# Four modulation chunks moved between the feature products, folded in a kept PSUM bank

## The reference

```python
mod = (silu(c) @ w_ada + b_ada).reshape(b, 6, D_MODEL)      # w_ada (1024, 6144)
sh1, sc1, g1, sh2, sc2, g2 = [mod[:, j] for j in range(6)]
proj = (x * (1.0 + sc1) + sh1) @ w_in                       # -> z, xbc, dt, rg_x, rg_gate, q, k, v, g
...                                                         # the three mixers
x  = layernorm(ALPHA * x + (1.0 + g1) * (mixers @ w_out))
h2 = x * (1.0 + sc2) + sh2                                  # router, top-2 experts
x  = layernorm(ALPHA * x + (1.0 + g2) * moe(h2))
```

## Time and profile before

| | us |
|---|---|
| median of 3 runs | 2025.87 (2024.02 to 2026.23) |
| the profiled execution | 2027.97 |
| its span in the trace | 2026.2 |
| PE busy | 1626.1 (80%) |
| DVE busy | 761.2 (38%) |
| ACT busy | 347.1 (17%) |
| DMA, mean over the span | 280 GB/s |

### The profile page before, as it was taken

One profiled execution on the slowest core, in us unless ns is written; L12 is line 12 of the kernel. 1 busy time (PEld: TensorE's weight loads), 2 busy tenths in 40 slices (PEclk: granted clock), 3 DMA queues, 4 the chain that ended last, 5 costly groups with the idle time before them and its releaser, 6 DMA issues.

```text
span 2026.2 us, 29151 instructions
## 1 busy us (share of the span) xinstructions
PE 1626.1 (80%) x11574; PEld 881.1 (43%) x11574; DVE 761.2 (38%) x1701; ACT 347.1 (17%) x791; POOL 113.7 (6%) x162
## 2 busy tenths in 40 slices
PE   4999999898866767767699999989886766777782
PEld 1775534443533333334277553344353433333341
DVE  0254636437522212222436364453762211222235
ACT  0235211102111110110123521110211110111000
POOL 3001012010100000000020000201000000000000
PEclk8899988859888878888979989895989888888896
DMA  9332344573699999999943243548259999999992
GB/s 331 115 126 75 99 140 135 180 278 149 253 427 427 429 428 428 429 429 428 391 153 125 88 125 86 174 163 299 101 243 427 427 429 428 428 428 429 429 427 96
DMA packets 93461, 567.51 MB, mean 280 GB/s; under 512 B 7061, under 2 KB 7917, under 8 KB 68034
## 3 DMA queue, kind: packets, MB, share of 16 engines
q1 hardware_dynamic: 81666, 532.06, 64.6%
q0 software_dynamic: 11712, 34.32, 6.1%
HBM read 550.54 MB, written 15.81 MB: 280 GB/s over the span
## 4 chain that ended last, share of the span: by engine, by line
PE 46%; DMA 37%; DVE 9%; issue 2%; ACT 2%; DVEq 2%; SPq 2%; POOL 0%; ACTq 0%; POOLq 0%
DMA ring<-in_exp_w_up 35%; PE ps L1367 10%; PE ps L894 8%; PE ps L918 8%; PE ps L1106 3%; PE ps L901 2%; PE ps L791 2%; PE ps L1056 1%; PE ps L1225 1%; PE ps L1181 1%; PE ps L1076 1%; PE ps L1342 1%; PE ps L1281 1%; DMA r0s<-in_state_ret 1%; DMA ring<-in_w_ada 1%
## 5 line engine op out<-in xcount | busy, mean ns | idle before, releaser
L1367 PE MATMUL ps<-ring,xTb 128*32 128x256 f32 x4224 | 328.6, 479 | 238.9 <-DMA ring<-in_exp_w_up 233.5
L1367 PEld LDWEIGHTS ps<-ring,xTb 128*32 128x32 f32 x4224 | 163.6, 137 | 403.3 <-issue 359.3
L2414 DVE TENSOR_TENSOR hb<-sg,ps 128x128 f32<-128x128 f32 x66 | 25.0, 379 | 493.0 <-ACT sg L1704 493.0
L918 PE MATMUL ps<-ring,hT 128*128 128x512 f32 x384 | 178.0, 621 | 0.0
L894 PE MATMUL ps<-hT,ring 128*128 128x288 f32 x640 | 163.6, 415 | 4.6 <-ACT hT L1487 3.5
L1342 PE MATMUL ps<-sel,h_tm 128*128 128x128 f32 (+1 forms) x912 | 163.2, 306 | 0.0
L1342 PEld LDWEIGHTS ps<-sel,h_tm 128*128 128x128 f32 x912 | 125.1, 189 | 53.8 <-issue 27.2
L894 PEld LDWEIGHTS ps<-hT,ring 128*128 128x128 f32 x640 | 122.7, 195 | 39.5 <-issue 6.5
L1381 PE MATMUL ps<-ring,hTb 128*32 128x256 f32 x2112 | 129.9, 387 | 6.0 <-DVEq L2417 3.8
L918 PEld LDWEIGHTS ps<-ring,hT 128*128 128x128 f32 x384 | 75.2, 200 | 107.4 <-issue 106.1
L1704 ACT ACTIVATE sg<-ps 128x128 f32<-128x128 f32 x66 | 18.3, 277 | 596.2 <-PE ps L1367 596.2
(11 more groups left out here) (412 smaller groups left out, 1750.5 us busy)
## 6 DMA issues: line engine op xcount, KB each, us to landing
ring<-in_exp_w_gate SPq DMA_DIRECT2D x66, 2048.0 KB, 18.8
ring<-in_exp_w_up SPq DMA_DIRECT2D x66, 2048.0 KB, 23.2
ring<-in_exp_w_down SPq DMA_DIRECT2D x66, 2048.0 KB, 24.7
ring<-in_w_ada SPq DMA_DIRECT2D x24, 2048.0 KB, 11.0
ring<-in_w_in SPq DMA_DIRECT2D x22, 2048.0 KB, 8.3
ring<-in_w_out SPq DMA_DIRECT2D x8, 2048.0 KB, 10.0
h0s<-in_state_ssd POOLq DMA_DIRECT2D x16, 512.0 KB, 6.9
out_ssd_s<-h0s POOLq DMA_DIRECT2D x16, 512.0 KB, 5.3
```

Of the source, the lines that this page charges most:

```text
L918: last = mm(o[:, :], hT[:, k, T0[i]:T0[i] + P], w[:, k, :], start=(k == 0), stop=(k == KT - 1))
L1367: last = mm(ps[32 * j:32 * j + 32, b, 0:2 * P], xTb[:, k, m * BLK:(m + 1) * BLK], w[:, 0:2, k * D_EXPERT + j * P:k * D_EXPERT + (j + 1) * ...
```

## The change

Chunks 4 to 7 leave the retention. Chunk 4, 5 and 6 are multiplied behind the feature products m = 3, 7 and 11 (and the transposes that follow these), chunk 7 behind the dt product and the state transposes, ahead of the gate products. Their ScalarE copies go to two places in turn (`spare`), so two by two they are folded at once: `fold_ada(4)` ahead of chunk 6 and `fold_ada(6)` behind the gate products add up the four strips with the constant `fold` and leave each chunk's 9 rows in a quarter (32 partitions) of PSUM bank 7. Bank 7 keeps all four until ScalarE copies it once, in the retention's second step, to `adaf`. `spread` then reads chunks 4 to 7 from 32 rows of `adaf`. Chunks 8 and 9 take the places of 4 and 5 at the end of `ret(1)`, 10 and 11 stand in the session loop behind b = 2 and b = 4. The ring's order and the bank plan follow.

```diff
-STREAM: ... + [("in", C_XBC + CH * n) for n in range(3)] + [("in", C_Z), ("in", C_Z + CH)] ... [("ada", n) for n in range(4, 12)] ...
+STREAM: ... + [x for n in range(3) for x in (("in", C_XBC + CH * n), ("ada", 4 + n))] + [("ada", 7)]
+          + [("in", C_Z), ("in", C_Z + CH)] ... [("ada", n) for n in range(8, 12)] ...
+        adaf = qkvg[:, 0, 0:CH]
@@ tensor: spread
-                        pe.wait_ge(*takes(l, ("ada", c)))
+                        if c < 8:
+                            pe.wait_ge(adaf_ready.sem, adaf_ready.at(l, 1))
+                        else:
+                            pe.wait_ge(*takes(l, ("ada", c)))
...
+                        lo, hi = (32 * (c - 4), 32 * (c - 3)) if c < 8 else (0, P)
+                        src = adaf[lo:hi, :] if c < 8 else ada_at(c)
+                        mm(o[:, :], C("fold", P, 0, 1)[lo:hi, :].to_broadcast([hi - lo, P]), src, start=True, stop=True
+                           ).then_inc(FL, 1)
+                def fold_ada(c):
+                    for j in (c, c + 1):
+                        pe.wait_ge(*takes(l, ("ada", j)))
+                    idle["pe"].stand(pe)
+                    for j in (c, c + 1):
+                        last = mm(ps[32 * (j - 4):32 * (j - 3), 7, :], C("fold"), ada_at(j), start=True, stop=True,
+                                  skip_group_check=True)
+                    return last
@@ tensor: features, behind the transposes of m
+                    if m in (3, 7, 11):
+                        if m == 11:
+                            fold_ada(4)
+                        ada(4 + m // 4, n)
+                        free_slot(n)
+                        n += 1
@@ tensor: behind the state transposes / behind the gate products
+                ada(7, n)
+                free_slot(n)
+                n += 1
+                fold_ada(6).then_inc(ada_folded.sem, 1)
@@ tensor: session loop; end of ret(1)
-                            if 1 <= b <= 6:
-                                ada_here(5 + b)
+                            if b in (2, 4):
+                                ada_here(9 + b // 2)
-                        ada_here(4)
-                        ada_here(5)
+                        ada_here(8)
+                        ada_here(9)
@@ scalar: in the feature loop; behind the tail copies; retention
+                    if m in (3, 7, 11):
+                        take_ada((4 + m // 4,))
+                take_ada((7,))
-                        take_ada(range(6, 12))
+                        take_ada((10, 11))
-                        take_ada((4, 5))
+                        act.wait_ge(ada_folded.sem, ada_folded.at(l, 1))
+                        cp(adaf, ps[:, 7, :]).then_inc(adaf_ready.sem, 1)
+                        take_ada((8, 9))
```

More of the change, by code:

```diff
@@ L73 @@
 STREAM = ([("ada", n) for n in range(4)] + [("in", C_RGX), ("in", C_RGG)]
-          + [("in", C_XBC + CH * n) for n in range(3)] + [("in", C_Z), ("in", C_Z + CH)]
-          + [("in", C_Q + CH * n) for n in range(4)] + [("out", 0), ("out", 1)]
-          + [("ada", n) for n in range(4, 12)] + [("out", 2), ("out", 3)])
+          + [x for n in range(3) for x in (("in", C_XBC + CH * n), ("ada", 4 + n))] + [("ada", 7)]
+          + [("in", C_Z), ("in", C_Z + CH)] + [("in", C_Q + CH * n) for n in range(4)] + [("out", 0), ("out", 1)]
+          + [("ada", n) for n in range(8, 12)] + [("out", 2), ("out", 3)])
 QUAD = 4
@@ L130, in ret_steps @@
             out.append((("rt", b), "D"))
-            if 1 <= b <= 6:
-                out.append((("ada", 5 + b), "A"))
+            if b in (2, 4):
+                out.append((("ada", 9 + b // 2), "A"))
     if i == 0:
@@ L138, in ret_steps @@
     if i == 1:
-        out += [(("ada", 4), "A"), (("ada", 5), "A")]
+        out += [(("ada", 8), "A"), (("ada", 9), "A")]
     return out
@@ L155, in bank_plan @@
             out.append((("xst", m - 3), "A"))
+        if m in (3, 7, 11):
+            out.append((("ada", 4 + m // 4), "A"))
     out += [(("tail", q), "A") for q in range((XT + RT) // 4)]
-    out += [(("dt",), "D"), (("h0rg",), "D")]
+    out += [(("dt",), "D"), (("h0rg",), "D"), (("ada", 7), "A")]
     out += [(("rga", m), "A") for m in range(RT)] + [(("rgi", m), "A") for m in range(RT)]
@@ L465, in trunk @@
         gate_used = sig("gate_used", 1)
+        ada_folded = sig("ada_folded", 1)
+        adaf_ready = sig("ada_folded_taken", 1)
         small_in = sig("small_in", 16 * 13)
@@ L807, in spread @@
                     for j, c in enumerate(cs):
-                        last = mm(o[32 * j:32 * j + TS, :], C("gs"), ada_at(c), start=True, stop=True, skip_group_check=True)
+                        lo, hi = (32 * (c - 4), 32 * (c - 3)) if c < 8 else (0, P)
+                        src = adaf[lo:hi, :] if c < 8 else ada_at(c)
+                        last = mm(o[32 * j:32 * j + TS, :], C("gs")[lo:hi, :], src, start=True, stop=True, skip_group_check=True)
                     last.then_inc(FL, 1)
+                def fold_ada(c):
[6 more added lines that the diff above has]
+                    return last
                 def free_slot(n):
@@ L1110, in ada_here @@
                 def ada_here(c):
-                    ada(c, n_ada + c - 4)
-                    free_slot(n_ada + c - 4)
+                    ada(c, n_ada + c - 8)
+                    free_slot(n_ada + c - 8)
                 for i in range(2):
@@ L1215, in _ @@
                 idle["pe"].stand(pe)
-                n = n_ada + 8
+                n = n_ada + 4
                 w = [stream(n), stream(n + 1)]
```

3 lines of the change are left out of this document (1 added, 2 removed).

## The result

The changed kernel took 2031.41 us, the median of 16 runs (2026.82 to 2040.08), against 2024.2 us for the kernel before in as many runs on the same chip (2018.11 to 2028.22): ratio 1.0036, 95% interval 1.0022 to 1.0050. It is slower, by a little more than the 0.2% that tell a change from none. It is 4.3 us above the forecast of 2027.1, and that understates the miss: the forecast had +1.2 us over the kernel before, and the medians of the sixteen runs stand 7.2 us apart. The profiled executions hide it: the one after took 2027.69 us (span 2025.7), the one before 2027.97 us (span 2026.2), one of the fastest of the one kernel and one of the slowest of the other.

A forecast was written before the change was run, and what follows sets the result against it. TensorE was taken to bound the mixer's feature products and half-clock session loop. Per layer 10.9 + 0.3 less 10.7 or 10.5 gave +1.2 us together, 2027.1 against the median 2025.87; range 2020 to 2035.

The forecast's parts named there:

- The likeliest case: Whole kernel: chunks cost in the features about what the session loop gives back, 2027.1 us; chance 0.48.
- Sessions without a chunk: Retention's session loop: a session that carries no chunk takes 4.33 us, DVE's chain setting the pace, clock at half.
- The wait for the states: Session loop: reloaded states come late at the last session, 0 to 0.5 us lost, 0.3 taken per layer.
- The features with the second fold: Feature stage up to z, both folds included: the moved chunks add 10.9 us per layer.
- Transposes to tails: Features' end, chunk 6 and first fold: 4.3 us after, 3.2 before, so 1.1 us is paid.
- Chunks 4 and 5: Behind feature products 3 and 7: each costs the full 2.57 us, 5.1 us for two.
- Chunk 7 at half clock, copy and table load exposed: Around the gate products: chunk 4.15 us at half clock, then 5.65 us of ACT's queue before the seventh gate product.
- z starts: Features' end: z's products begin 11.7 us after chunk 7 begins, second fold included, against 7.0 before.
- Rival (b): z products: clock falls after the stall before the seventh gate product; 3.3 us per layer, 2033.7, one layer 2030.4; chance 0.22.
- I take 0, nearest to the row: Spread of chunks 4 and 5 after the session loop: reading 32 rows instead of 128 changes nothing in sum.
- Both of its bounds: Spread of chunks 4 and 5: products side by side win 1.6 us; a clock returning later costs 1.7.
- The spread of 6 to 9 lies beside DVE's LayerNorm and counts for nothing: Later spread of modulation chunks 6 to 9: it runs beside DVE's work, so its change adds 0 us.

## Why the prediction came out as it did

The likeliest case (an even exchange, within 0.2%) did not come; the time is 0.36 and 0.30% above the kernel before, inside the range given and on its slower side. The stages give +5.0 us where the forecast had +1.2. By the steps:

- Sessions without a chunk, 4.33 us, DVE next: right, in all four layers. The wait for the states: right in kind, hidden in part behind what DVE had taken; the loop gave 0.4 us per layer more than forecast.
- The features with the second fold: +11.8 for +10.9. Transposes to tails: right (4.21 against 4.3). Chunks 4 and 5: the products behind chunk 5 lie 2.73 us later against those ahead of it, where 2.57 was forecast. Chunk 7 at half clock, copy and table load exposed: right in both layers (the seventh gate product 9.81 and 10.09 us after chunk 7's start, forecast 9.80), though its wait is 2.43 or 0.72 us depending on the gates' own clock. That z starts 11.6 and 11.2 us behind chunk 7 for 11.7 is a match by the mark alone, as the fold lies behind it and not ahead.
- Rival (b), the clock falling behind that wait: it came in layer 0, where the wait was the longer, and not in layer 1. The last gate products took 1.79 us there and 1.14 in layer 1, fold and z together 3.77 (172.03 to 175.80) and 2.77. The price was some 1.7 us, not 3.3, since the clock was 0.98 from 174 on. That the measured 2031.4 lies near this rival's 2030.4 for one layer is luck: most of the loss is elsewhere.
- The step that failed: "I take 0, nearest to the row", for the spread and what stands behind it. Both of its bounds came true at once: the products side by side (2.08 us for 3.31) and the later clock, under which the sample rows took 1.92 for 1.05 and the first output products 5.64 for 3.70. -1.23 + 0.87 + 1.94 is +1.6 in layer 0; in layer 1 it was +1.0. And "The spread of 6 to 9 lies beside DVE's LayerNorm and counts for nothing" failed with it: +0.3 in each layer. Together 1.6 per layer on average, 3.2 of the 5.0 us. The bound of 1.7 for the later clock rested on 3.4 us of output products at half clock, a length that no row gave. The run with all rows wide returns half of the 1.6.
- The stage from z to the scores holds the fold (+0.84) and is otherwise unchanged: 201.29 and 201.32 us in layer 1 against 200.51. In layer 0 it varies by 7 us between executions. The score stage's +0.1 is +1.5 in layer 1 and -1.4 in layer 0, where the clock had fallen in the trace before.
- Between the 5.0 us of the stages and the 6.0 and 7.2 us of the two pairs of medians 1 to 2 us stay open; the stages were read in one and two executions.
- Why it turned slower and not even: the run with chunk 7 behind the gates has all the rest of the change, the narrow spread too, and the time of before. The change is even except for chunk 7's place, which costs 2.6 us per layer at the features' end, and some 1 in the score stage; how the 2.6 divide between the half clock and ACT's queue no run shows.

## What to carry to other kernels

A piece of work moved between two stretches of a bound engine gains only the difference of its prices, so find the place where the clock is up and no other engine's queue has something to do behind its copy: here the same chunk cost 2.56 us behind the gates and 4.23 ahead of them, plus a table load. Before filling an idle stretch of one engine, follow the chain of the engine it waits for to the end of the stage; if the next wait is for the same line, the gap is slack and filling it wins nothing. And a change of a few tenths of a per cent is not read from one trace of each kernel: add up stages over layers and executions, and expect that the clock of a distant stretch may move more than the edit.

## What the runs showed of the hardware

- Products of 32 rows in different row strips ran side by side: four took 2.08 us, where the same four over 128 rows took 3.78 us, both at half clock. The Trainium skill, "TensorE: Matmul & The Clock Gate", Part 3, says so, and the runs agree. It did not carry over to the sample rows' products where half of them read 32 rows and half 128: eight took 2.03 us at full clock, and 1.06 or 1.07 with all at 128 rows.
- Behind the narrow products the granted clock stayed at half into the first output products (5.64 us for eight, 3.70 behind wide ones); changing only four of the eight back to 128 rows brought it forward (3.70 in both layers) and won nothing in sum.
- The gather behind the router took 9.02 us or 14.90 us for 48 products, at a granted clock of 0.92 or 0.50, with the only edit 150 us ahead of it.
- A state of 256 KB, loaded in 3.6 us in the changed kernel's loop, with one ring load beside it (median of five), took 7.7 us in a loop with four ring loads (median of four).
